# Expert turns of a two-layer trunk on TensorE: the gather of the next turn placed behind the down matmuls, the scatter of a turn behind the gate and up matmuls of the next

## What is computed

```python
def moe(h, l, p):
    scores = jax.nn.sigmoid(jnp.einsum('bld,de->ble', h, p['w_router'], preferred_element_type=f32))
    ...
    gate = jnp.sum(jax.nn.one_hot(idx, N_EXPERTS, dtype=f32) * w[..., None], axis=-2)
    hg = jnp.einsum('bld,edf->blef', h, p['w_gate'][l])
    hu = jnp.einsum('bld,edf->blef', h, p['w_up'][l])
    act = jax.nn.silu(hg) * hu
    return jnp.einsum('blef,ble,efd->bld', act, gate.astype(act.dtype), p['w_down'][l])
```

## Time and profile before

| | us |
|---|---|
| median of 3 runs | 1154.87 (1153.7 to 1157.39) |
| the profiled execution | 1154.73 |
| its span, first to last instruction | 1152.9 |
| TensorE matmul busy | 1001.4 (87%) |
| DVE busy | 434.2 (38%) |
| ACT busy | 178.0 (15%) |
| TensorE's mean granted clock | 0.914 of full |

### The profile page before, as it was taken

One profiled execution on the slowest core, in us unless ns is written; L12 is line 12 of the kernel. 1 busy time (PEld: TensorE's weight loads), 2 busy tenths in 40 slices (PEclk: granted clock), 3 DMA queues, 4 the chain that ended last, 5 costly groups with the idle time before them and its releaser, 6 DMA issues.

```text
span 1152.9 us, 13566 instructions
## 1 busy us (share of the span) xinstructions
PE 1001.4 (87%) x5248; PEld 538.8 (47%) x5248; DVE 434.2 (38%) x781; ACT 178.0 (15%) x446; POOL 68.0 (6%) x114
## 2 busy tenths in 40 slices
PE   4698997788779999999979999886687999999996
PEld 1354553555664334444435455464575344444442
DVE  1167656541332222222236666555133221222222
ACT  2120003331200011101123000332211011011001
POOL 4402200002000000000000121000000000000000
PEclk8798998968869999999988999897695999999999
DMA  9967554334609999999962764322070899999991
GB/s 360 298 257 258 184 187 173 137 111 109 258 1 372 406 408 406 412 411 412 406 230 103 261 221 146 146 78 92 5 261 32 334 405 409 402 412 407 408 410 57
DMA packets 67726, 299.32 MB, mean 260 GB/s; under 512 B 8344, under 2 KB 18712, under 8 KB 38992
## 3 DMA queue, kind: packets, MB, share of 16 engines
q1 hardware_dynamic: 61952, 291.52, 64.3%
q0 software_dynamic: 2656, 4.30, 1.7%
q10 hardware_dynamic: 3056, 2.64, 0.7%
HBM read 295.81 MB, written 2.62 MB: 259 GB/s over the span
## 4 chain that ended last, share of the span: by engine, by line
PE 72%; DVE 13%; ACT 6%; issue 5%; POOL 2%; ACTq 1%; DMA 0%; DVEq 0%; POOLq 0%
PE ps L386 70%; PE ps L419 2%; ACT eP L1375 2%; DVE rt L905 1%; DVE proj L1336 1%; DVE stat L905 1%; DVE eP L1170 1%; ACT proj L1598 1%; DVE eP L1168 1%; DVE F L1021 1%; ACT hnT L1433 1%; DVE xs L1124 0%; DVE t L1355 0%; DVE x L1358 0%; ACT stat L1380 0%
## 5 line engine op out<-in xcount | busy, mean ns | idle before, releaser
L386 PE MATMUL ps<-ring,proj 128*64 128x512 f32 x1536 | 336.7, 594 | 15.3 <-ACT proj L1598 15.3
L386 PE MATMUL ps<-ring,hnT 128*128 128x512 f32 (+1 forms) x576 | 212.2, 523 | 16.9 <-DVE proj L1057 9.2
L386 PEld LDWEIGHTS ps<-ring,proj 128*64 128x64 f32 x1536 | 112.7, 137 | 216.0 <-issue 210.4
L386 PEld LDWEIGHTS ps<-ring,hnT 128*128 128x128 f32 x576 | 110.9, 198 | 98.8 <-issue 75.4
L386 PE MATMUL ps<-hnT,ring 128*64 128x256 f32 (+1 forms) x640 | 89.9, 400 | 12.6 <-DMA rbias<-in_router_bias 10.5
L1331 DVE TENSOR_SCALAR proj<-proj 128x512 f32<-128x512 f32 x16 | 6.8, 427 | 206.6 <-ACT proj L1375 206.6
L386 PEld LDWEIGHTS ps<-hnT,ring 128*64 128x64 f32 (+1 forms) x640 | 62.7, 155 | 38.8 <-DMA rbias<-in_router_bias 10.6
L386 PEld LDWEIGHTS ps<-proj,xs 128*128 128x128 f32 x512 | 59.7, 192 | 7.7 <-issue 7.7
L1342 DVE COPY proj<-ps 128x512 f32<-128x512 f32 x16 | 11.1, 691 | 135.1 <-PE ps L386 135.1
L386 PE MATMUL ps<-proj,xs 128*128 128x128 f32 x512 | 59.8, 275 | 0.0
L386 PE MATMUL ps<-ring,silT 128*32 128x512 f32 x384 | 51.7, 666 | 9.2 <-DVE silT L920 9.2
(11 more groups left out here) (248 smaller groups left out, 836.7 us busy)
## 6 DMA issues: line engine op xcount, KB each, us to landing
ring<-in_w_gate SPq DMA_DIRECT2D x64, 1024.0 KB, 10.8
ring<-in_w_up SPq DMA_DIRECT2D x64, 1024.0 KB, 11.3
ring<-in_w_down SPq DMA_DIRECT2D x64, 1024.0 KB, 7.7
ring<-in_w_ada SPq DMA_DIRECT2D x48, 1024.0 KB, 9.4
ring<-in_w_in SPq DMA_DIRECT2D x28, 1024.0 KB, 7.0
ring<-in_w_out SPq DMA_DIRECT2D x16, 512.0 KB, 4.0
ring<-in_w_in SPq DMA_DIRECT2D x4, 512.0 KB, 14.2
x<-in_x_prompt POOLq DMA_DIRECT2D x1, 512.0 KB, 9.3
```

The costliest lines, as they stand in the source:

```text
L386: ins = nc.tensor.matmul(*a, **k)
```

## The change

TensorE's steps are put in two functions, `gather(t)` and `scatter(t)`. Gather 0 stands ahead of the turns; in turn t the order is gate and up, scatter of turn t-1 (from t = 1 on), transposes, down, gather of turn t+1 (up to t = 6); scatter 7 stands behind the turns. DVE builds `seat` of the next turn in the present one, once the present gather has read it, and `seatG` once the last turn's transposes have read it. The gather now pays owed slot releases too. The ring keeps its eight slots; SP's and ACT's lists are as before.

```diff
-                    for t in range(TURNS):
+                    def gather(t):
+
                         led.turn = t
...
                                     last = mm(ps[:, half, k * P:(k + 1) * P], rows[:, g, KH * half + k, :], seat[:, g, :], start=(g == 0), stop=(g == 1))
+                                    if not (k == KH - 1 and g):
+                                        pay(last)
                             last.then_inc(c.fills(half, "xT", half), 1)
+
+                    def scatter(t):
+
+                        led.turn = t
+                        pe.wait_ge(c.of("seatTs"), c.at("seatTs"))
+                        for h in range(2):
+                            pe.wait_ge(c.of("ys", h), c.at("ys", h))
+                            for g in range(NG):
+                                last = pay(mm(ps[:, 4 + 2 * g + h, :], seatT[:, g, :], ys[:, h, :], start=False, stop=False, skip_group_check=True))
+                        return last
+
+                    gather(0)
+                    for t in range(TURNS):
+                        led.turn = t
...
+                        if t:
+                            scatter(t - 1)
+                            led.turn = t
                         pe.wait_ge(c.of("seatG", 0), c.at("seatG", 0))
...
-                        pe.wait_ge(c.of("seatTs"), c.at("seatTs"))
-                        for h in range(2):
-                            pe.wait_ge(c.of("ys", h), c.at("ys", h))
-                            for g in range(NG):
-                                pay(mm(ps[:, 4 + 2 * g + h, :], seatT[:, g, :], ys[:, h, :], start=False, stop=False, skip_group_check=True))
+                        if t + 1 < TURNS:
+                            gather(t + 1)
+                    scatter(TURNS - 1)
...
+                    def seats(t):
+
+                        led.turn = t
+                        if t:
+                            led.turn = t - 1
+                            dve.wait_ge(c.of("xT", 1), c.at("xT", 1))
+                            led.turn = t
+                        for g in range(NG):
+                            st(tt(by_seat(seat, g), C["slot"][:].rearrange("p (o s) -> p o s", o=1).broadcast_to([P, 2, SLOTS]), at(seatno, g), ALU.is_equal), "seat", g - 1)
+
+                    seats(0)
                     for t in range(TURNS):
                         led.turn = t
...
+                        if t:
+                            led.turn = t - 1
+                            dve.wait_ge(c.of("seatT"), c.at("seatT"))
+                            led.turn = t
                         for g in range(NG):
                             st(tt(by_seat(seatG, g), by_seat(seat, g), at(gt, g), ALU.mult), "seatG", g - 1)
+                        if t + 1 < TURNS:
+                            seats(t + 1)
+                            led.turn = t
```

More of the change, by code:

```diff
@@ L1319, in _, with at @@
                     step[0] = "dve_turn"
+                    by_seat = lambda a, g: a[:, g].rearrange("p (e s) -> p e s", e=2)
+                    def at(a, g):
+                        t = led.turn
+                        return a[:, g, t * 2:t * 2 + 2].rearrange("p (e o) -> p e o", o=1).broadcast_to([P, 2, SLOTS])
+                    def seats(t):
[7 more added lines that the diff above has]
+                    seats(0)
                     for t in range(TURNS):
                         led.turn = t
[L1323 to L1326, removed]
+                        if t:
+                            led.turn = t - 1
+                            dve.wait_ge(c.of("seatT"), c.at("seatT"))
+                            led.turn = t
                         for g in range(NG):
                             st(tt(by_seat(seatG, g), by_seat(seat, g), at(gt, g), ALU.mult), "seatG", g - 1)
+                        if t + 1 < TURNS:
+                            seats(t + 1)
+                            led.turn = t
                         dve.wait_ge(c.of("gexp"), c.at("gexp"))
```

## The result

| | before | changed |
|---|---|---|
| median of 4 runs, us | 1156.13 | 1142.24 (1140.76 to 1146.24) |
| ratio to before | | 0.9886 (0.9851 to 0.9922) |
| profiled execution, its span | 1154.73, 1152.9 | 1140.84, 1139.0 |

A second set of runs of the same two kernels gave 0.9882 (0.9858 to 0.9907), 1142.09 against 1155.14 us, 13.1 us; against before_again, the same kernel before run once more, with 1153.60 us, it is 11.5.

A forecast was written before the change was run, and what follows sets the result against it. TensorE was taken to set the turn, with transfers following closely. Only covering the `act` wait counted, other terms 0: 1154.73 - 7.3 = 1147.4, with 0.14 for the median 1147.6 us; range 1144.5 to 1152.

The forecast's parts named there:

- the wait for `act`: TensorE ahead of the `act` transposes: seven of eight waits go, 3.65 us a layer; turn 0 keeps 0.45.
- the wait for the copy of `actT`: TensorE behind the `act` transposes, waiting for ACT's copy: unchanged, near 7.3 us a layer.
- Two of the signs: Expected in the changed profile: turns of 30.0 to 30.4 us, and a transfer rate of 415 to 418 GB/s.
- cost of the register instructions: Register instructions now within the gather: cost 0, at worst 0.1 us each, bound 1.4 us.
- the term for the scatter behind up: Previous turn's scatter between up and the transposes hides 0.52 us of idle TensorE a turn; 7.3 us over two layers.
- start-to-start sum: A turn's TensorE steps from gate and up to gather, added start to start: 30.31 us, where before 30.83.
- a change of tiling mode drains TensorE: Drain behind up, no longer beside a wait: would count against the change, but already held in the rows' times.
- Transfers that eat the gain: Rival: weight transfers become the bound and take most or all of the gain, 1151.5 to 1155 us; chance 0.15.
- Two dry spells: Rival: DMA engines run dry twice a turn, 1.1 us each, 31.9 us of transfers a turn, 1166 us; chance 0.05.
- My working of the ring's timing: Slot release, landing and use times in a turn: weights land before they are wanted; loss taken as 0.
- the 2 us of slack ahead of the up weights: Narrowest place: up weights issued at 23.1 us land by 35 and are wanted at 37.2.
- That `act` is late for another reason: Rival at the activation: the change uncovers nothing, since more than DVE's 0.70 us delays it; answered no, no chance given.

The follow-up runs named there:

- act_first: Changed kernel with the four `act` transposes ahead of the two `seatG` transposes; 1140.91 us, ratio 0.9898 to the kernel before.
- scatter_split: Changed kernel with the scatter in two halves, one behind up, one beside ACT's copy; 1140.46 us, ratio 0.9897 to the kernel before.
- seat_late: Changed kernel, but DVE forms the next turn's seats behind its copy of the second down bank, as before; 1167.27 us, ratio 1.0098 to the kernel before.
- the padded kernels: Kernel before and changed kernel, each with two extra matmuls of zeros behind layer 0's last turn; 1152.10 and 1143.76 us.
- old_order: Changed kernel with TensorE's old order, scatter of turn t behind down of turn t; 1153.22 us, ratio 0.9993 to the kernel before.
- after_half_down: Changed kernel with half of each down transfer left out, for timing only; 1140.88 us, 29.96 us a turn.
- the four kernels above: Kernel before, changed kernel, and each with two extra matmuls of zeros between the layers; 1156.13, 1142.24, 1152.10 and 1143.76 us.

## Why the prediction was wrong

**Direction and mechanism** held. TensorE set the turn, the scatter covered the wait for `act`, turn 0 kept its 0.45, the wait for the copy of `actT` stayed at 7.3 us in layer 0, the transfers followed. Two of the signs came out beyond their bounds: turns of 29.95 us where I had 30.0 to 30.4, and 421 GB/s where I had 415 to 418. No cost of the register instructions shows: turns still differ by the same 0.1 to 0.4 us as before.

**The step that failed is the term for the scatter behind up, 0.52 us a turn, measured 0.74**, 10.3 us and not 7.3 over fourteen turns. Three pieces of my own start-to-start sum were mis-sized:

- I carried the two `seatG` transposes at 0.44 us, the length of their group when it stands alone. In the new order all six transposes run on behind one another, and from the scatter's end at 386.95 to ACT's copy at 387.90 it is 0.95 us. The four of `act` take 0.72 of it, as act_first shows, so the two cost 0.23, **0.21 less** than I took. The 0.23 us is also what they give back when act_first moves them beside the copy (1.59 - 1.36). Alone they start 0.16 us apart and their bar runs on behind the second; in the row the next one starts 0.11 us behind each.
- I carried the `act` transposes and the copy at 1.77 us, of which 0.84 go by up to the copy's start. In the row it is 0.72, **0.12 less**. Behind the wait for `act` the first transpose's weights were loaded only when it started (the weight loads of before, first row); behind the scatter they were loaded 0.43 us ahead, while the scatter's last matmul ran (act_first, second row). In turn 0 of act_first, where the wait stands, it is 0.85 again.
- I carried the gather at 3.66 us. Right behind down it takes 369.52 - 365.76 = 3.76, in every turn, **0.10 more**. All of it lies between its first two matmul instructions, 0.21 us apart where before they were 0.11. Here too the first weights were loaded 0.43 us ahead when the scatter stood in front (third row, gather at 402.06), and are loaded at the start behind down (fourth row).

```profile
451.49 0.56 PEld L419 LDWEIGHTS ps<-c_ident,proj 128*128 128x128 f32 x4 [0.76 <-DVE proj L1336]
```
```profile
448.30 0.20 PEld L419 LDWEIGHTS ps<-c_ident,proj 128*128 128x128 f32 x1 [0.24 <-issue]
```
```profile
401.63 0.19 PEld L386 LDWEIGHTS ps<-proj,xs 128*128 128x128 f32 x1 [0.24 <-issue]
```
```profile
365.75 0.52 PEld L386 LDWEIGHTS ps<-proj,xs 128*128 128x128 f32 x4 [0.81 <-issue]
```

0.52 + 0.21 + 0.12 - 0.10 = 0.75, the measured 0.74. That the late first load is what costs the 0.10 to 0.12 us is read from where these rows stand; no run changed it by itself.

Of the Trainium skill's rule that a change of tiling mode drains TensorE (TensorEngine Tiling (Array Packing), Key Properties) I had said that the rows hold its price behind up, and they did: gate and up take 13.89 us from their start to that of the scatter (383.41 - 369.52), as they took 13.88 to that of the transposes. It could bear on the gather's 0.10, behind the 64-column pairs of down, and on the half of the scatter that scatter_split puts behind up, which takes 445.71 - 443.88 = 1.83 us where the half behind transposes takes 447.89 - 446.18 = 1.71. But in seat_late the gather starts after 1.51 us without a matmul behind down and takes the same 3.77 (401.67 to 405.44), so a wait for the array to drain is not what costs it there.

**The sum left out what is not the change's.** I put everything outside the turns at nothing. Of the 13.1 to 13.9 us 2.8 to 3.6 lie there: 1.6 to 2.1 between the layers, which repeat with the kernel but come, as the padded kernels show, from the moment at which the matmuls start again and not from the scatter's place; 0.4 the other way behind the last turn, in old_order too; and the rest is the start up to the first down, which wanders by 2 us and more from trace to trace. That the 2 us between the layers came on top of the gain is luck: seat_late, act_first and scatter_split, with the same new order, did not get them. Below, my range allowed 0.2 us more a turn, for issue time, and nothing for what lies outside the turns. With the turn at 0.74 and the mixer unmoved the forecast would have been 1144.6, just inside the range; the stretch between the layers took the time out of it.

**The rivals.** Transfers that eat the gain: not at eight slots, as after_half_down shows; but 0.15 us a turn further they do bind, as scatter_split shows. By the Trainium skill (DMA: Bandwidth & Descriptors, Where 436 GB/s comes from) the HBM side binds at about 358 GB/s; here 421 was sustained over 149 us, and the measurement decides. Two dry spells: not at eight slots, but seen at six. My working of the ring's timing, on which I put the 2 us of slack ahead of the up weights, gave no loss at six slots and is refuted there, so that number had no ground to stand on, and that I was right about the transfers at eight slots was in part luck. That `act` is late for another reason, so that nothing is gained: no, the wait went in all turns but the first.

## What to carry to other kernels

A stall is cured best by a step whose inputs are a stage old, and such a move often needs a second, gainless one (here DVE's seats, worth 22 us when missing) to keep the place it leaves covered. Before sizing a reordering, price a short group by start to next start within a row of its kind, not by its own bar beside a wait: here the row saved 0.33 us a turn over the bars. And when the DMA engines' share reads about 1.00 on both sides, take bytes away from one of them: where the turn stays, it was the other.

## What was not expected of the hardware

In these traces the granted clock after the pause between the layers is at 0.50, 1.2 GHz, and comes back to full 2.8 to 5.0 us behind the first matmul in the four kernels above; shifting that start by 1.7 us exchanges the two cases. Up to layer 1's first down this was worth 2 us in a kernel of 1140, more than some edits. What sets the moment was not tried. From 154 to 160 us the granted clock had a mean of 0.72 (with single microseconds at 0.50) in one execution while matmuls ran without a gap, and stayed full in another. Two kernels that differ by a few us in one place can therefore differ by 2 more in a place they share, and only a trace tells.
